# Tokens leave PSUM as two one-pass halves, and the spatial gate's product runs in three one-pass products

## The chip, the cores and the metric

The kernel runs on one core of one Trainium2 chip. The metric is device time in microseconds (us). The kernel before takes 4471.25 us, the median of 3 runs (4468.71 to 4473.4). The profiled execution took 4474.2 us, and its trace spans 4472.3 us.

## The reference

The reference is a small model on 1024 tokens of width 1024, all in f32: a first block with three mixers and an MLP, then an even layer, an odd layer, and a mixture of experts behind each. The change touches the stretch from the end of the first block's mixers to the projections of the even layer. In the reference's words:

```
x = x + gt_m * (merged @ w_out[l])
h = rms_norm(x, norm_mlp_g[l]) * (1.0 + sc_f) + sh_f
x = x + gt_f * (jnp.square(jax.nn.relu(h @ mlp_w1[l])) @ mlp_w2[l])
return rms_norm(x, final_norm_g)          # end of the first block
```

The even layer normalizes that x once more and multiplies it with one wide matrix. 512 of its columns go through a GELU and a spatial gate (a product over tokens), the other 2304 are the queries, keys and values of 12 attention heads, with a rotation of some columns. Both products take the same turned tokens h.

## The kernel before

**Stages.** The program is a row of stages. Each is a block with one instruction list per engine, written out in the order in which the engine runs it. `Stage.__exit__` (line 47) ends each with a barrier of all engines, so no engine starts a stage before the last engine has ended the one before. There is no scheduler: the source sets the order, and semaphores (`wait_ge`, `then_inc`) tie the engines.

**One product, two ways.** Tokens are turned by TensorE (a transpose of 128x128 tiles with the identity), since a product needs its contraction on the partitions. A product of f32 operands as they are is one `matmul` per tile. The other way is `split` (line 143) and `three_passes` (line 150): each operand is cast to fp32r (its high half) and the rest (its low half) is subtracted from it; then high times high, high times low and low times high are added up in PSUM, each with an fp32r `matmul`.

```
def three_passes(pe, out, left, right, start, stop):
    (lh, ll), (rh, rl) = left, right
    pe.matmul(out, lh, rh, start=start, stop=False)
    pe.matmul(out, lh, rl, start=False, stop=False)
    return pe.matmul(out, ll, rh, start=False, stop=stop)
```

**The stretch of the change**, stage by stage:

- `out_norm_stage` as "out" (lines 1725 to 1926): for each of 8 token tiles, 48 matmuls with `w_out`, the gate and the sum on VectorE, the norm, 8 transposes into PSUM (`out_th`), and a copy by ScalarE into `m["hT"]` as f32 (line 1857). The MLP's first weights are loaded here ahead of time (`mlp_ahead`).
- `mlp_stage` (lines 1942 to 2154): VectorE first splits the whole of `m["hT"]` (128x8192), then the first weights (128x4096), and TensorE waits for both (`h_split`, `w_split`). Then 8 turns, each with 8 tiles of `hidden` (24 matmuls) and 16 of `output` (12 matmuls). In the last turn the norms for the even layer ride along: `add`, `mean`, `inverse` on VectorE, squares and roots on ScalarE, 8 transposes for each token tile on TensorE (`turn_h`), and a copy by ScalarE into `m["hT"]` (lines 2078 and 2082).
- `spatial_stage` (lines 2157 to 2225): 8 tiles of 8 f32 matmuls each, `m["hT"]` times one weight slot of 128x4096 (line 2187), a GELU on ScalarE for each tile, then the norm of the gate on VectorE, four products over tokens (line 2195) and four gates.
- `gemm_stage` as "even" (lines 552 to 714): VectorE splits `m["hT"]` in four pieces and, after the first piece, the first of six sets of weights (128x3072 each), which is loaded at the start of this stage. TensorE runs 48 tiles of 24 matmuls of 384 columns, and turns queries and keys one tile late (line 647), when VectorE has rotated them (`x_ready`).

**Names.** `m["hT"]` and `m["hT_r"]`, `m["oN"]` and `m["oN_r"]`, `ring` and `ring_r` are each one piece of memory under an f32 and an fp32r name. The ring has four slots of 128x4096. SP's queue carries the loads, POOL's the stores.

## Time and profile before

| what | us |
|---|---|
| median of 3 runs | 4471.25 |
| the profiled execution | 4474.2 |
| its span in the trace | 4472.3 |
| TensorE busy, share of the span | 3847.5, 86% |
| VectorE busy | 2588.4, 58% |
| ScalarE busy | 1653.6, 37% |

The stretch of the change, from the trace (busy time inside each window):

| window, us from the start | what runs | TensorE busy | VectorE busy | ScalarE busy | granted clock |
|---|---|---|---|---|---|
| 1213 to 1326 | out | 98.67 | 65.29 | 34.48 | 0.94 |
| 1326 to 1347 | split of tokens and weights, MLP | 0.14 | 19.75 | 0.03 | 0.50 |
| 1347 to 2002 | the MLP up to its last outputs | 655.00 | 365.95 | 38.24 | 1.00 |
| 2002 to 2065 | last outputs with norms | 53.60 | 46.30 | 28.25 | 0.93 |
| 2065 to 2124 | spatial: the f32 product | 57.23 | 0.00 | 6.35 | 0.96 |
| 2124 to 2141 | spatial: the gate | 5.80 | 12.70 | 1.45 | 0.70 |
| 2141 to 2153 | split of tokens and weights, even | 0.00 | 8.29 | 0.00 | 0.68 |
| 2153 to 2370 | the even projections | 214.69 | 72.83 | 36.48 | 0.99 |

The granted clock is TensorE's, as a share of full speed (0.50 is 1.2 GHz, 1.00 is 2.4 GHz). Busy time tells which engine works; what ends a stretch is read from the idle time in front of an instruction and from the engine that ended it.

### The profile page before, as it was taken

How to read it: one execution, taken by the hardware profiler on the slowest of the kernel's cores; microseconds unless marked ns; L12 is line 12 of the kernel's file. 1: busy time of each engine (PE TensorE's matmuls, PEld its weight loads, DVE VectorE, ACT ScalarE, POOL GpSimd, SP SyncE). 2: the span in 40 equal slices, each digit the busy share in tenths (PEclk: the TensorE clock that was granted, in tenths of full speed). 3: DMA queues.
4: the chain of work that ended last, by engine and by line, in shares of the span. 5: the costliest groups of instructions: out<-in, count | busy, mean ns of one | idle time of the engine just before them, and what ended most of it. 6: DMA issues, size and time to landing. Idle time of an engine off the chain costs nothing. (4 is left out here: it accounts for less than half of the span.)

```text
span 4472.3 us, 56432 instructions
## 1 busy us (share of the span) xinstructions
PE 3847.5 (86%) x22256; PEld 3122.2 (70%) x22256; DVE 2588.4 (58%) x3982; ACT 1653.6 (37%) x2226; POOL 493.3 (11%) x471
## 2 busy tenths in 40 slices
PE   5988998977989999998797998599677798993996
PEld 2766877866767888885796876377566687872775
DVE  6356772068755555553524763677565465745775
ACT  2223342155420000003114762367513465732675
POOL 0001122000000000000230000133103000000341
PEclk9989999989999999999898999799888899996998
DMA  7101113230531111111313103399603202032997
GB/s 293 48 22 62 62 64 104 71 126 33 177 134 38 38 56 50 44 66 42 113 46 139 38 26 137 127 374 370 206 16 96 68 20 112 13 115 98 355 371 274
DMA packets 136489, 518.88 MB, mean 116 GB/s; under 512 B 17952, under 2 KB 70336, under 8 KB 118224
## 3 DMA queue, kind: packets, MB, share of 16 engines
q1 hardware_dynamic: 101936, 411.94, 25.1%
q0 software_dynamic: 31216, 101.85, 7.2%
q8 instruction: 149, 2.44, 0.2%
q10 hardware_dynamic: 3120, 2.10, 0.2%
q14 instruction: 68, 0.56, 0.0%
HBM read 427.21 MB, written 88.62 MB: 115 GB/s over the span
## 5 line engine op out<-in xcount | busy, mean ns | idle before, releaser
L2052 ACT ACTIVATE mlp_relu<-mlp_z 128x512 f32<-128x512 f32 x64 | 38.3, 598 | 637.7 <-PE mlp_z L155 637.7
L3106 DVE TENSOR_TENSOR ring_r<-ring,oN_r 128x4096 fp32r<-128x4096 f32 x48 | 212.2, 4424 | 67.8 <-ACT oN_r L3037 67.7
L153 PE MATMUL scans_G<-ring_r 128*128 128x512 f32 x544 | 221.8, 408 | 32.3 <-ACT scans_stg L2560 18.3
L3106 DVE TENSOR_TENSOR ring_r<-ring,hT_r 128x4096 fp32r<-128x4096 f32 x48 | 212.3, 4423 | 59.3 <-ACT hT_r L3037 59.3
L153 PE MATMUL mlp_z<-ring_r,mlp_w_high_r 128*128 128x512 f32 x512 | 200.0, 391 | 21.9 <-DVE ring_r L147 21.9
L3037 ACT ACTIVATE oN_r<-ring 128x4096 fp32r<-128x4096 f32 x48 | 174.0, 3629 | 82.2 <-DMA ring<-in_w_all 67.6
L3037 ACT ACTIVATE hT_r<-ring 128x4096 fp32r<-128x4096 f32 x48 | 174.0, 3628 | 70.2 <-DMA ring<-in_w_all 70.2
L155 PE MATMUL mlp_z<-ring_r 128*128 128x512 f32 x512 | 199.7, 390 | 0.0
L154 PE MATMUL mlp_z<-hT_r,mlp_w_high_r 128*128 128x512 f32 x512 | 199.6, 390 | 0.0
L153 PE MATMUL mlp_y_ps<-mlp_w_high_r,oN_r 128*128 128x512 f32 x512 | 199.6, 390 | 0.0
L155 PE MATMUL mlp_y_ps<-mlp_w_high_r,oN_r 128*128 128x512 f32 x512 | 199.2, 389 | 0.0
L154 PE MATMUL mlp_y_ps<-ring_r,oN_r 128*128 128x512 f32 x512 | 199.2, 389 | 0.0
L154 PE MATMUL scans_G<-hT_r,ring_r 128*128 128x512 f32 x480 | 191.7, 399 | 0.0
L155 PE MATMUL scans_G<-ring_r 128*128 128x512 f32 x480 | 191.1, 398 | 0.0
L2924 POOL TENSOR_TENSOR moe_taker<-moe_zero 128x1 f32<-128x1 f32 x64 | 135.9, 2124 | 438.4 <-ACT moe_y L3096 425.9
L2099 DVE TENSOR_TENSOR mlp_relu<-mlp_relu 128x512 f32<-128x512 f32 x64 | 44.2, 691 | 184.8 <-ACT mlp_relu L2052 184.8
L2110 DVE TENSOR_TENSOR mlp_y<-mlp_y_ps,mlp_gt 128x512 f32<-128x512 f32 x128 | 88.2, 689 | 103.6 <-PE mlp_y_ps L155 101.3
L153 PEld LDWEIGHTS scans_G<-ring_r 128*128 128x128 f32 x544 | 104.9, 193 | 59.1 <-issue 14.8
L153 PE MATMUL even_gemm_acc<-even_gemm_w_high,even_gemm_h_high 128*128 128x384 f32 x384 | 133.9, 349 | 13.4 <-DVE ring_r L147 13.4
L1257 DVE CUSTOM_DVE_ANT_0 even_sc<-even_scores,even_table 128x1024 f32<-128x1024 f32 x96 | 117.0, 1220 | 23.3 <-issue 23.3
L154 PE MATMUL even_gemm_acc<-ring_r,even_gemm_h_high 128*128 128x384 f32 x384 | 130.1, 339 | 0.0
L155 PE MATMUL even_gemm_acc<-even_gemm_w_high,hT_r 128*128 128x384 f32 x384 | 129.8, 338 | 0.0
(645 smaller groups left out, 10654.9 us busy)
## 6 DMA issues: line engine op xcount, KB each, us to landing
ring<-in_w_all SPq DMA_DIRECT2D x118, 2048.0 KB, 10.7
ring<-in_w_mlp SPq DMA_DIRECT2D x16, 2048.0 KB, 7.7
ring<-in_w_all SPq DMA_DIRECT2D x12, 1024.0 KB, 6.3
branch_gates<-scans_stg POOLq DMA_DIRECT2D x48, 256.0 KB, 2.3
merge_raw<-branch_gates SPq DMA_DIRECT2D x16, 768.0 KB, 5.1
ring<-in_w_even SPq DMA_DIRECT2D x6, 1536.0 KB, 8.2
qk_turned<-even_gemm_y POOLq DMA_DIRECT2D x48, 128.0 KB, 2.3
even_qk<-qk_turned SPq DMA_DIRECT2D x6, 1024.0 KB, 5.1
```

Source lines behind the costliest of these rows:

```text
L153: pe.matmul(out, lh, rh, start=start, stop=False)
L154: pe.matmul(out, lh, rl, start=False, stop=False)
L155: return pe.matmul(out, ll, rh, start=False, stop=stop)
L1257: dve.tensor_tensor_reduce(out=sc[:, u % 3, :], in0=SA[:, 2 * (u % 2):2 * (u % 2) + 2, :].rearrange("p a n -> p (a n)"), in1=table[:, c:c ...
L2052: act.activation(r[:, n % 2, :], Z[:, n % 4, :], ACT.Relu).then_inc(z_free, 1)
L2099: step(dve.tensor_tensor(r[:, n % 2, :], r[:, n % 2, :], r[:, n % 2, :], ALU.mult))
L2110: dve.tensor_tensor(y[:, n % 2, :], Y[:, n % 4, :], gt[:, cols], ALU.mult).then_inc(y_free, 1)
L2924: pool.tensor_tensor(taker[:, n:n + 1], zero[:], zero[:], ALU.add)
L3037: act.activation(w_high[n % RING], buf[:, (first + n) % RING, :], ACT.Copy).then_inc(w_cast, 1)
L3106: dve.tensor_tensor(buf_r[:, b, :], buf[:, b, :], w_high[n % RING].bitcast(F32), ALU.subtract)\
```

## The change

1. In "out" (`halves=True`), ScalarE casts the turned tile from PSUM to fp32r into `m["oN_r"]`, and VectorE subtracts that from PSUM into `m["hT_r"]` (`low_h`). The f32 copy goes away. The next transposes wait for VectorE now.
2. In `mlp_stage` the split of the tokens is gone. The first weights are split in four quarters, the cast on ScalarE and the rest on VectorE, and TensorE's first tile waits for a quarter at each second k. The hidden layer's halves lie in ring slots 2 and 3 (they were in `m["oN_r"]`).
3. In the last turn of the MLP the tokens leave PSUM as halves too: `cast_h` on ScalarE, `low_h` on VectorE.
4. `spatial_stage` takes these halves, splits its weight slot in four quarters on ScalarE and VectorE, and runs 24 fp32r matmuls per tile in place of 8 f32 ones. It also loads the even layer's first weights into ring slot 1.
5. `gemm_stage` is left for "even" alone. The split of the tokens is gone; the first weights, in memory by then, are split in two halves on ScalarE and VectorE. Two of four weight buffers are new memory (`even_more`).

The diff, cut to its core:

```diff
 # out_norm_stage, ScalarE
                 if t >= 2:
                     act.wait_ge(h_turned, t - 1)
-                    act.activation(m["hT"][:, :, toks(t - 2)], TH[:, :, :], ACT.Copy).then_inc(h_taken, 1)
+                    if halves:
+                        act.wait_ge(o_split, t - 1)
+                        act.activation(m["oN_r"][:, :, toks(t - 2)], TH[:, :, :], ACT.Copy).then_inc(h_cast, 1)
 ...
 # out_norm_stage, VectorE
+            def low_h(i):
+                dve.wait_ge(h_cast, i + 1)
+                dve.tensor_tensor(m["hT_r"][:, :, toks(i)], TH[:, :, :], m["oN_r"][:, :, toks(i)].bitcast(F32), ALU.subtract)\
+                   .then_inc(h_taken, 1)
 ...
                 if t + 1 < NT:
                     low_o(t + 1)
+                if halves and t >= 2:
+                    low_h(t - 2)
                 if t < NT:
                     add(t, 0)
+            if halves:
+                low_h(NT - 1)
 # mlp_stage, TensorE
-            pe.wait_ge(h_split, 1)
 ...
                     for k in range(KD):
+                        if n == 0 and k % 2 == 0:
+                            pe.wait_ge(first_split, k // 2 + 1)
 # mlp_stage, ScalarE
+            act.wait_ge(m["mlp_w_in"][0], 16)
+            for j in range(4):
+                act.activation(quarter(w_high, j), quarter(buf, j), ACT.Copy).then_inc(w_cast, 1)
 # mlp_stage, VectorE
-            split(step, dve, m["hT"][:, :, :], h_high, h_low[:, :, :]).then_inc(h_split, 1)
-            dve.wait_ge(m["mlp_w_in"][0], 16)
-            split(step, dve, buf[:, 0, :], w_high[:, 0, :], buf_r[:, 0, :]).then_inc(w_split, 1)
+            dve.nop().then_inc(w_split, 1)
+            for j in range(4):
+                dve.wait_ge(w_cast, j + 1)
+                dve.tensor_tensor(quarter(buf_r, j), quarter(buf, j), quarter(w_high, j).bitcast(F32), ALU.subtract)\
+                   .then_inc(first_split, 1)
             dve.wait_ge(x_in, 32)
 ...
                 if 1 <= t <= NT:
                     mean(t - 1, 1)
+                if t >= 3:
+                    low_h(t - 3)
 # spatial_stage
+            sp.dma_start(buf[:, 1, 0:EVEN_W], m["w_even"][0, :, :]).then_inc(m["even_in"], 16)
 ...
-                    ins = pe.matmul(Z[:, t % 4, :], m["hT"][:, k, t * P:(t + 1) * P], w[:, k, :],
-                                    start=k == 0, stop=k == KD - 1)
+                    if t == 0 and k % 2 == 0:
+                        pe.wait_ge(w_split, k // 2 + 1)
+                    ins = three_passes(pe, Z[:, t % 4, :], [h[:, k, t * P:(t + 1) * P] for h in (h_high, h_low)],
+                                       [v[:, k, :] for v in w], k == 0, k == KD - 1)
 # gemm_stage, VectorE
-            for q in range(4):
-                toks = slice(q * 2 * P, (q + 1) * 2 * P)
-                split(step, dve, m["hT"][:, :, toks], h_high[:, :, toks], h_low[:, :, toks]).then_inc(h_split, 1)
-                if q == 0:
-                    split_w(0)
+            for j in range(2):
+                dve.wait_ge(w_cast, j + 1)
+                dve.tensor_tensor(half(w_low[0], j), half(w_raw[0], j), half(w_high[:, 0, :], j).bitcast(F32), ALU.subtract)\
+                   .then_inc(first_split, 1)
```

VectorE's list from the last norm of "out" into the MLP (`out_h` is the normed tile, `hT_r` the low half of the tokens, `ring_r` in the first of these rows the high half), before:

```order
L1917 SCALAR_TENSOR_TENSOR out_h<-out_x,out_rs,out_gain 128x1024
L1921 TENSOR_TENSOR out_h<-out_h,out_shift 128x1024
L36 UNCONDITIONAL_BRANCH
L2084 UNCONDITIONAL_BRANCH
L146 CAST ring_r<-hT 128x8192
L147 TENSOR_TENSOR hT_r<-hT,ring_r 128x8192
L146 CAST mlp_w_high_r<-ring 128x4096
L147 TENSOR_TENSOR ring_r<-ring,mlp_w_high_r 128x4096
```

and with the change:

```order
L1898 SCALAR_TENSOR_TENSOR out_h<-out_x,out_rs,out_gain 128x1024
L1902 TENSOR_TENSOR out_h<-out_h,out_shift 128x1024
L1887 TENSOR_TENSOR hT_r<-out_th,oN_r 128x8x128 x2
L37 UNCONDITIONAL_BRANCH
L2083 UNCONDITIONAL_BRANCH
L2090 TENSOR_TENSOR ring_r<-ring,mlp_w_high_r 128x1024 x4
```

Two subtractions of one tile each stand before the stage's end, and four of a quarter behind it, in place of two instructions over all tokens and two over all of the weights.

VectorE's list at the end of the MLP (`mlp_w_high` is where the normed tile lies, `mlp_z` the PSUM of the transposes), before:

```order
L2117 TENSOR_SCALAR mlp_ss<-mlp_ss 128x1
L2122 RECIPROCAL mlp_rs<-mlp_rs 128x1
L2145 SCALAR_TENSOR_TENSOR mlp_w_high<-mlp_x,mlp_rs,mlp_w_high 128x1024
L36 UNCONDITIONAL_BRANCH
L2207 UNCONDITIONAL_BRANCH
L377 TENSOR_TENSOR spatial_sq<-spatial_z 128x2048
```

and with the change:

```order
L2118 TENSOR_SCALAR mlp_ss<-mlp_ss 128x1
L2139 TENSOR_TENSOR hT_r<-mlp_z,ring_r 128x8x128
L2123 RECIPROCAL mlp_rs<-mlp_rs 128x1
L2152 SCALAR_TENSOR_TENSOR mlp_w_high<-mlp_x,mlp_rs,mlp_w_high 128x1024
L2139 TENSOR_TENSOR hT_r<-mlp_z,ring_r 128x8x128 x2
L37 UNCONDITIONAL_BRANCH
L2229 UNCONDITIONAL_BRANCH
L2234 TENSOR_TENSOR ring_r<-ring,spatial_w_high 128x1024 x4
L378 TENSOR_TENSOR spatial_sq<-spatial_z 128x2048
```

One subtraction has come between the last mean and its reciprocal, two behind the last norm, and four quarters of weights into the stage that follows.

SP's queue where the spatial stage meets the even projections, before:

```order
L2176 DMA spatial_bs<-in_b_spatial 128x4
L36 UNCONDITIONAL_BRANCH
L587 UNCONDITIONAL_BRANCH
L592 DMA ring<-in_w_even 128x3072
L600 DMA even_gemm_cos<-in_cos_even 128x64
```

and with the change:

```order
L2190 DMA spatial_bs<-in_b_spatial 128x4
L2191 DMA ring<-in_w_even 128x3072
L37 UNCONDITIONAL_BRANCH
L579 UNCONDITIONAL_BRANCH
L582 DMA ring<-in_w_even 128x3072
L586 DMA even_gemm_cos<-in_cos_even 128x64
```

The first weights' load stands one stage earlier, and the second weights' load is the first of the stage now.

## Rows read from the trace of the kernel before

**Rows 1.** Timeline, out's end to MLP: start us, us, engine, line, tile [idle before <-releaser].

```profile
1305.02 0.69 DVE L1891 TENSOR_TENSOR out_h<-out_y_ps,out_gate 128x512 f32<-128x512 f32 x1 [3.11 <-PE out_y_ps L155]
1323.00 1.97 PE L1811 MATMUL out_th<-identity,out_h 128*128 128x128 f32 x8 [5.35 <-DVE out_h L1921]
1325.01 1.02 ACT L1857 ACTIVATE hT<-out_th 128x1024 f32<-128x1024 f32 x1 [4.83 <-PE out_th L1811]
1326.98 4.43 DVE L146 CAST ring_r<-hT 128x8192 fp32r<-128x8192 f32 x1 [4.04 <-PEq L39]
1331.45 8.69 DVE L147 TENSOR_TENSOR hT_r<-hT,ring_r 128x8192 fp32r<-128x8192 f32 x1
1342.38 4.42 DVE L147 TENSOR_TENSOR ring_r<-ring,mlp_w_high_r 128x4096 fp32r<-128x4096 f32 x1
1346.86 0.80 PE L153 MATMUL mlp_z<-ring_r,mlp_w_high_r 128*128 128x512 f32 x1 [21.88 <-DVE ring_r L147]
1348.30 0.63 PE L153 MATMUL mlp_z<-ring_r,mlp_w_high_r 128*128 128x512 f32 x1
1348.73 0.63 PE L154 MATMUL mlp_z<-hT_r,mlp_w_high_r 128*128 128x512 f32 x1
1354.08 0.60 ACT L2052 ACTIVATE mlp_relu<-mlp_z 128x512 f32<-128x512 f32 x1 [28.05 <-PE mlp_z L155]
1359.52 0.60 ACT L2052 ACTIVATE mlp_relu<-mlp_z 128x512 f32<-128x512 f32 x1 [4.84 <-PE mlp_z L155]
```

**Rows 2.** Timeline of the merge stage: prices of casts and subtractions.

```profile
1118.56 1.05 ACT L1373 ACTIVATE merge_w_high<-ring 128x1024 fp32r<-128x1024 f32 x1
1209.37 1.49 ACT L1385 ACTIVATE merge_raw<-merge_raw 128x1536 f32<-128x1536 f32 x1 [4.47 <-DMA merge_raw<-branch_gates]
1129.09 1.23 DVE L1398 TENSOR_TENSOR ring_r<-ring,merge_w_high 128x1024 fp32r<-128x1024 f32 x1
1130.23 1.22 DVE L1393 TENSOR_TENSOR hT_r<-merge_tp,merge_o_high 128x1024 fp32r<-128x1024 f32 x1
1131.37 0.68 DVE L1416 TENSOR_TENSOR oN<-merge_raw,merge_up 128x512 f32<-128x512 f32 x1
```

**Rows 3.** Issues of the MLP's start: KB, us from issue to landing.

```profile
mlp_x<-x_rows SPq DMA_DIRECT2D x1, 4096.0 KB, 13.1
```

**Rows 4.** Timeline, the last outputs of the MLP.

```profile
2042.30 0.69 DVE L2110 TENSOR_TENSOR mlp_y<-mlp_y_ps,mlp_gt 128x512 f32<-128x512 f32 x1 [1.15 <-PE mlp_y_ps L155]
2060.23 0.15 DVE L2117 TENSOR_SCALAR mlp_ss<-mlp_ss 128x1 f32<-128x1 f32 x1 [1.22 <-ACT mlp_relu L2062]
2060.66 0.16 DVE L2122 RECIPROCAL mlp_rs<-mlp_rs 128x1 f32<-128x1 f32 x1 [0.27 <-ACT mlp_rs L2067]
2064.20 1.02 ACT L2082 ACTIVATE hT<-mlp_z 128x1024 f32<-128x1024 f32 x1 [2.66 <-PE mlp_z L2030]
```

**Rows 5.** Timeline, the spatial product.

```profile
2066.01 1.28 ACT L2202 ACT_TABLE_LOAD   x1 [0.79 <-PEq L39]
2066.05 9.16 PE L2187 MATMUL spatial_z_ps<-ring,hT 128*128 128x512 f32 x16 [1.89 <-PEq L39]
2123.32 0.60 ACT L2202 ACTIVATE spatial_z<-spatial_z_ps 128x512 f32<-128x512 f32 x1 [6.27 <-PE spatial_z_ps L2187]
```

**Rows 6.** Timeline, the start of the even projections.

```profile
2141.57 1.23 DVE L146 CAST even_gemm_h_high<-hT 128x2048 fp32r<-128x2048 f32 x1 [0.77 <-PEq L39]
2153.45 0.66 PE L153 MATMUL even_gemm_acc<-even_gemm_w_high,even_gemm_h_high 128*128 128x384 f32 x1 [13.44 <-DVE ring_r L147]
2160.41 0.49 ACT L659 ACTIVATE oN<-even_gemm_acc 128x384 f32<-128x384 f32 x1 [31.29 <-PE even_gemm_acc L155]
2164.57 0.49 ACT L659 ACTIVATE oN<-even_gemm_acc 128x384 f32<-128x384 f32 x1 [3.67 <-PE even_gemm_acc L155]
2170.62 0.44 PE L647 MATMUL even_gemm_tp<-identity,oN 128*128 128x128 f32 x2 [1.40 <-DVEq L714]
```

**Rows 7.** Windows: us, PE, PEld, DVE, ACT, POOL busy, granted clock, DMA, GB/s.

```profile
2145.00:2146.00 1.00, 0.00 (x0) 0.00 (x0) 0.12 (x1) 0.00 (x0) 0.00 (x0) 0.65 1.09 467
```

More of the change, by code:

```diff
@@ L549, in take_turned, with gemm_stage @@
         act.activation(dst[:, ks, t * P:(t + 1) * P], psum[:, t % 2, ks, :], ACT.Copy).then_inc(free, 1)
-def gemm_stage(nc, m, kind):
-    with Stage(nc, f"{kind}_gemm") as st:
-        even = kind == "even"
-        NS, WIDE, NB = (6, 3 * P, 2) if even else (2, 3 * P + 64, 3)
+def gemm_stage(nc, m):
+    with Stage(nc, "even_gemm") as st:
+        NS, WIDE, NB = 6, 3 * P, 2
         N, SIZE, HEADS = NS * NT, KD * WIDE, 2 * NB
         VW = WIDE - NB * P
-        buf, buf_r = (t_[:, :, 0:SIZE] for t_ in (m["ring"].buf, m["ring"].buf_r))
-        h_high = st.sb("h_high", [P, KD, S], F32R)
-        h_low = m["hT_r"]
+        more, more_r = twin_buffer(nc, st.ctx, "even_more", [P, 2, SIZE])
+        w_raw, w_low = ([t_[:, b, 0:SIZE] for b in (1, 0)] + [u_[:, b, :] for b in range(2)]
+                        for t_, u_ in ((m["ring"].buf, more), (m["ring"].buf_r, more_r)))
+        h_high, h_low = ring_halves(m), m["hT_r"]
@@ L1722, in _, with out_norm_stage @@
             step(dve.tensor_tensor(o, sq, g_sub[:, :].unsqueeze(1).unsqueeze(1).to_broadcast([P, NT, H, P]), ALU.mult))
-def out_norm_stage(nc, m, name, src, gain, gate=None, scale=None, shift=None, turned=range(KD), keep=None, ahead=None, o_turned_in=None):
+def out_norm_stage(nc, m, name, src, gain, gate=None, scale=None, shift=None, turned=range(KD), keep=None, ahead=None, o_turned_in=None,
+                   halves=False):
     with Stage(nc, name) as st:
@@ L2199, in _ @@
         def _(act):
+            m["ring"].wait(act, first)
+            for j in range(4):
+                act.activation(quarter(w_high, j), quarter(buf[:, slot, :], j), ACT.Copy).then_inc(w_cast, 1)
             for t in range(NT):
@@ L2209, in _ @@
             step = Steps(dve, stepped)
+            for j in range(4):
+                dve.wait_ge(w_cast, j + 1)
+                dve.tensor_tensor(quarter(buf_r[:, slot, :], j), quarter(buf[:, slot, :], j),
+                                  quarter(w_high, j).bitcast(F32), ALU.subtract).then_inc(w_split, 1)
             dve.wait_ge(par_in, 48)
```

143 lines of the change are left out of this document (67 added, 76 removed).

## The prediction

> **What bounds the kernel now.** I read the page's busy shares first (the table ahead of this), then busy time by window, then the timeline of each engine around the four places the diff touches. The chain of waits is of no use here, since it names only the last stage. TensorE is busy 86% of the span. Inside the MLP, in "out" and in the even projections it hardly waits, so VectorE and ScalarE have room there and their work costs nothing. In three places TensorE stands and VectorE works alone. (a) Between "out" and the MLP TensorE waits 21.88 us, and what ends that wait is the last subtraction of the weights' split; before it VectorE has cast and subtracted all tokens, 4.43 and 8.69 us [rows 1]. (b) At the even projections it waits 13.44 us for the same kind of work [rows 6]. (c) Once more it waits 1.40 us for a rotated tile [rows 6]. A fourth place is of another kind: the f32 product of the spatial stage has TensorE busy from 2066.05 until the last GELU starts at 2123.32, 57.27 us [rows 5], with ScalarE and VectorE nearly idle. Between any two stages lies a barrier, so every microsecond at these places is a microsecond of the kernel.
>
> **The end of "out", +2.4 us.** Before, the last 8 transposes start at 1323.00, when the normed tile is ready, the copy starts at 1325.01 and takes 1.02, and the stage ends at 1326.03 [rows 1]. Now two subtractions of 128x1024 stand behind the last norm. The first belongs to tile 6, and the last transposes wait for it, since there is one buffer in PSUM. The subtraction of that very form, PSUM minus fp32r half, takes 1.22 us in the merge stage, and the next instruction starts 1.14 after it started [rows 2]. So the transposes start about 1.15 later; then come 2.01, the cast with 1.02, and the second subtraction with 1.22 plus a few hundredths for the handover. The stage ends at 1326.03 + 1.15 + 1.24, 2.39 later. The other six subtractions lie where VectorE waits for TensorE; in each round of "out" it waits 3.11 us (the row at 1305.02) [rows 1], and nothing that TensorE needs in that round comes later by more than the subtraction's 1.14.
>
> **The start of the MLP, -17.5 us.** Before: 20.83 us from the end of "out" (1326.03) to the first matmul (1346.86) [rows 1]. Now: the barrier, 0.95 (1326.03 to 1326.98) [rows 1]; ScalarE's cast of the first quarter, 128x1024, 1.05 [rows 2]; VectorE's subtraction, 1.23 [rows 2]; two handovers of about 0.05, of which the one to TensorE is read in [rows 1] (1342.38 + 4.42 to 1346.86). Together 3.3. The other quarters come every 1.14, and TensorE needs 6 matmuls at 0.43 for one at its low clock [rows 1], so it doesn't wait for them. The barrier is not removed. What is late next is the load of the MLP's x. It starts 2.4 later, with the stage, takes 13.1 us [rows 3], and VectorE waits for it ahead of its first square. So it is ready near 1343, some 3 to 4 us after the first relu (1331.8 + 7.22 = 1339.0, with 7.22 from the first matmul to the first relu [rows 1]). Behind this wait stand VectorE's splits of the hidden layer, and behind these ScalarE's third relu (two buffers are free at the start) and TensorE's seventh tile. Tiles come 5.44 apart (1354.08 to 1359.52) [rows 1], so TensorE asks for that at about 1331.8 + 7.2 + 5 x 5.44 = 1366. Cost nothing, with 20 us to spare.
>
> **The last turn of the MLP, +2.0 us.** VectorE gets one more subtraction in each of six rounds. In a full round it is idle for 1.15 us ahead of the next round's product (the row at 2042.30) [rows 4]. The step of 1.14 fits, with next to nothing left. I take 0; 0.3 a round (a step of 1.4) in five rounds would be 1.5 us. The Trainium skill speaks against a fit: "VectorE: DVE Perf Modes", the section on the TRN2 errata, gives a Vector instruction 120 cycles of fixed cost with a PSUM source and 58 with an SBUF source, 62 cycles at 0.96 GHz, 65 ns more. The trace does not bear that out for this form: 1.22 us from PSUM beside 1.23 from SBUF [rows 2]; by the rule the sum would change by no more than 0.3 us. At the end: the last mean starts at 2060.23, the reciprocal at 2060.66 [rows 4]. Now the subtraction of tile 5 comes between and holds VectorE until 2060.23 + 0.07 + 1.14 = 2061.44, so the last norm, transposes and cast come 0.78 later, and behind the cast (2064.20 + 1.02 [rows 4]) comes the last subtraction, 1.22 and a handover: 0.78 + 1.25 = 2.03.
>
> **The spatial product, -9.6 us.** A tile is now 24 fp32r matmuls of 512 columns, which is what a tile of the MLP's hidden layer is: 5.44 us, and 7.22 from the first matmul to the first relu, with the slow clock of the start in it [rows 1]. Eight tiles: 7.22 + 7 x 5.44 = 45.3, in place of 57.27. The stage also starts with a quarter's cast and subtraction ahead of TensorE, 2.33 (its weights have been in memory since the MLP). -11.97 + 2.33 = -9.64. The GELU's table load of 1.28 [rows 5] moves behind the casts and stays hidden by the first tile. The gate behind it is untouched. The slow start could be as long as that of the even projections, whose first tile takes 6.96 and the second 4.16 [rows 6], 2.8 more; in the MLP it is 1.8 more. So -8.6 is the other end.
>
> **The even projections, -8.5 and -1.4 us.** Before: 11.88 us from the stage's first instruction (2141.57) to the first matmul (2153.45) [rows 6]. Now ScalarE casts a half of 128x1536: 1.49, by the activation of that size, and VectorE subtracts it: 1.23 for 1024 and 4.42 for 4096 columns [rows 1, 2] give 1.76 for 1536. With handovers 3.34. -8.54. The load of these weights lies in the spatial stage, beside 45 us of matmuls. The second half is ready 1.8 us after the first, and TensorE needs 12 matmuls for the first, about 3.5 us. The wait of 1.40 [rows 6] came from VectorE being busy with tokens until after the first tile; now the first rotation starts when its tile is there, and the split of the second weights, 5.1 us long, ends about a microsecond before TensorE asks for the second rotated tile (after its third tile, 2 x 4.16 behind the first). Gone: -1.40, at worst 0. The load of the second weights is issued at the stage's start and has landed by then, as the first weights had in 6.6 us before. One thing can give more: in the window 2145 to 2146 the granted clock falls, 0.65 on average [rows 7], and TensorE's first matmul would now come at 2144.9 on this time scale. If the clock holds, the slow start goes, up to 2.5 us of the 2.8. I leave it in, since the fall and the start are within half a microsecond.
>
> **The sum.** 2.4 - 17.5 + 2.0 - 9.6 - 8.5 - 1.4 = -32.6 us. Against its own time of 4474.2 the profiled execution would take 4441.6; it stands 3.0 above the median of the runs (4471.25), and the same difference against the median gives 4438.6. I say 4439 us, 0.73% faster. About 0.2%, 9 us, is what a measurement of this kernel can tell from no change.
>
> **Rivals.**
> - *VectorE bounds the MLP's last rounds, and the slow starts are long.* For it: 1.14 into 1.15 us. Against: the step is measured on the same form. It gives +1.5, +1.0 in the spatial product, and the 1.40 stays: 4442.5.
> - *The clock holds into the even projections.* -2.5: 4436. For it: TensorE's matmuls of the gate end nearly 5 us before, and the fall comes just then. Against: the fall comes first if nothing else sets it.
> - *The waits move rather than go.* The splits go, but TensorE then stands for the MLP's x, or for weights that have not landed, for 10 to 15 us more. Against: the room of 20 us above, weights loaded a stage ahead. It would give about 4450.
> - *Slower: TensorE stays at its low clock.* With shorter pauses and more matmuls the granted clock might not rise in the spatial product and the first of the even weight sets. Price: a matmul of 512 columns 0.43 apart (1348.30 to 1348.73 [rows 1]) in place of 0.227 (5.44 / 24), 0.20 more, for 192 of them +39; and 192 of 384 columns at about 0.15 more, +28. That gives 4438.6 + 67 less the slow starts counted already, about 4502. It decides from about 160 matmuls at the low clock against the gain of 32.6, and 205 for slower by over 0.2%. Against: at each start in this trace the clock rises within the first tile.
> - *The change doesn't do what it says*, for example VectorE is still what TensorE waits for because quarters come too slowly: each would cost at most 0.1 us by the steps above.
>
> **How the numbers follow.** Forecast 62%, with its own range 4434 to 4444 (measurement 2.5 either way, 2 for the ends of the terms); VectorE and long starts 12%, clock holds 15%, waits moved 8% (half of it within the range below), low clock 3%. Range 4431 to 4448: it leaves out the worst of the moved waits, the low clock and a tail on the fast side, under 2 in 10. Faster by over 0.2% (under 4462): 0.94; within: 0.03; slower by over 0.2%: 0.03.
>
> **What would show it.** TensorE's wait ahead of the MLP's first matmul falls from 21.9 to about 5.7, with the transposes' wait ahead of it up from 5.35 to 6.5; 13.4 ahead of the even projections becomes about 5; the spatial product's last GELU starts some 45 us after its first matmul; no wait of 1.4 at the second turned tile; VectorE's idle time in the MLP's last rounds near zero at an unchanged distance of rounds. I am wrong if the rounds of "out" or of the MLP's last turn grow longer, if TensorE waits for a hidden tile's relu in the first turn, or if a stage that the diff does not touch moves.

## The result, and the profile after

The changed kernel takes 4441.36 us, the median of 4 runs (4439.74 to 4450.08), beside 4472.32 for the kernel before (4 runs, 4468.71 to 4478.27). The ratio is 0.9933, with a 95% interval of 0.9916 to 0.9951. The forecast was 4439, range 4431 to 4448. The profiled execution took 4439.74 us. Its page says of span and busy time:

```profile
span 4437.9 us, 56597 instructions
PE 3831.2 (86%) x22320; PEld 3131.0 (71%) x22320; DVE 2581.3 (58%) x3994; ACT 1662.6 (37%) x2236; POOL 499.9 (11%) x471
```

The shares are those of before. What moved can be seen only at the four places. Timeline of the changed kernel from the end of "out" into the MLP (start us, us, engine, line, tile, then the idle time before and what ended it), the counterpart of [rows 1]:

```profile
1319.96 1.94 PE L1783 MATMUL out_th<-identity,out_h 128*128 128x128 f32 x8 [6.58 <-DVE hT_r L1887]
1321.93 1.02 ACT L1831 ACTIVATE oN_r<-out_th 128x1024 fp32r<-128x1024 f32 x1 [6.03 <-PE out_th L1783]
1322.99 1.23 DVE L1887 TENSOR_TENSOR hT_r<-out_th,oN_r 128x1024 fp32r<-128x1024 f32 x1 [3.18 <-ACT oN_r L1831]
1325.08 3.90 ACT L2044 ACTIVATE mlp_w_high_r<-ring 128x1024 fp32r<-128x1024 f32 x4 [2.13 <-PEq L40]
1326.17 4.63 DVE L2090 TENSOR_TENSOR ring_r<-ring,mlp_w_high_r 128x1024 fp32r<-128x1024 f32 x4 [1.96 <-ACT mlp_w_high_r L2044]
1327.54 0.77 PE L154 MATMUL mlp_z<-oN_r,mlp_w_high_r 128*128 128x512 f32 x1 [5.65 <-DVE ring_r L2090]
1339.49 0.69 DVE L2100 TENSOR_TENSOR mlp_relu<-mlp_relu 128x512 f32<-128x512 f32 x1 [8.69 <-DMA mlp_gt<-mod_rows]
```

TensorE waited 21.88 us ahead of the MLP's first matmul and now waits 5.65. Its last transposes waited 5.35 and now wait 6.58, for the subtraction that the change put ahead of them. The last row is the wait for the MLP's x and gate.

Timeline of VectorE in one of the MLP's last rounds, and of the stage's end, the counterpart of [rows 4]:

```profile
2008.36 0.15 DVE L2118 TENSOR_SCALAR mlp_ss<-mlp_ss 128x1 f32<-128x1 f32 x1
2008.43 1.21 DVE L2139 TENSOR_TENSOR hT_r<-mlp_z,ring_r 128x1024 fp32r<-128x1024 f32 x1
2009.67 0.69 DVE L2111 TENSOR_TENSOR mlp_y<-mlp_y_ps,mlp_gt 128x512 f32<-128x512 f32 x1
...
2041.30 1.22 DVE L2139 TENSOR_TENSOR hT_r<-mlp_z,ring_r 128x1024 fp32r<-128x1024 f32 x1
2042.43 0.15 DVE L2123 RECIPROCAL mlp_rs<-mlp_rs 128x1 f32<-128x1 f32 x1
2042.62 1.28 DVE L2152 SCALAR_TENSOR_TENSOR mlp_w_high<-mlp_x,mlp_rs,mlp_w_high 128x1024 f32<-128x1024 f32 x1
2047.02 1.23 DVE L2139 TENSOR_TENSOR hT_r<-mlp_z,ring_r 128x1024 fp32r<-128x1024 f32 x1 [1.98 <-ACT ring_r L2068]
```

The subtraction of 1.21 stands where VectorE was idle for 1.15, and the product behind it (2009.67) starts with no bracket, so with no idle time. At the end the subtraction at 2041.30 stands between the mean and its reciprocal.

Timeline of the spatial product, the counterpart of [rows 5]:

```profile
2051.46 0.79 PE L154 MATMUL spatial_z_ps<-spatial_w_high,ring_r 128*128 128x512 f32 x1 [5.53 <-DVE ring_r L2234]
2096.97 0.60 ACT L2224 ACTIVATE spatial_z<-spatial_z_ps 128x512 f32<-128x512 f32 x1 [4.84 <-PE spatial_z_ps L156]
```

From its first matmul to its last GELU are 45.5 us instead of 57.3. Timeline and windows (us; PE, PEld, DVE, ACT and POOL busy; granted clock) of the start of the even projections, the counterpart of [rows 6, 7]:

```profile
2119.05 0.66 PE L154 MATMUL even_gemm_acc<-even_gemm_w_high,ring_r 128*128 128x384 f32 x1 [4.96 <-DVE ring_r L672]
2125.43 0.49 ACT L651 ACTIVATE oN<-even_gemm_acc 128x384 f32<-128x384 f32 x1 [6.94 <-PE even_gemm_acc L156]
2129.60 0.49 ACT L651 ACTIVATE oN<-even_gemm_acc 128x384 f32<-128x384 f32 x1 [3.67 <-PE even_gemm_acc L156]
```

```profile
2115.00:2116.00 1.00, 0.00 (x0) 0.00 (x0) 0.00 (x0) 0.37 (x1) 0.00 (x0) 1.00 0.00 0
2116.00:2117.00 1.00, 0.00 (x0) 0.00 (x0) 0.00 (x0) 1.00 (x1) 0.00 (x0) 0.70 0.70 123
2117.00:2118.00 1.00, 0.00 (x0) 0.00 (x0) 0.85 (x1) 1.00 (x2) 0.00 (x0) 0.50 0.52 184
```

The wait of 13.44 is 4.96, and no turned tile is waited for. In the MLP's last turn the transposes of two neighbouring tiles are 6.81 us apart, as before, and the tiles of "out" 11.8 us, as before: the rounds did not grow. The clock falls between 2116 and 2117, before the first matmul at 2119.05.

**A table of steps.** The stretch of the change can be cut at instructions that all kernels have. The numbers are differences of start times (an end, where it says end) in the profiled executions, in us:

| from the row before to | before | after | predicted change | measured change |
|---|---|---|---|---|
| end of "out", from ScalarE's take of tile 6 (counted from 0) | 8.34 | 10.80 | +2.39 | +2.46 |
| MLP's first matmul | 20.83 | 3.32 | -17.5 | -17.51 |
| first relu | 7.22 | 7.53 | 0 | +0.31 |
| last relu | 647.36 | 647.36 | 0 | 0 |
| end of the MLP | 63.78 | 65.82 | +2.03 | +2.04 |
| last GELU | 58.10 | 48.72 | -9.64 | -9.38 |
| end of the gate | 17.47 | 17.91 | 0 | +0.44 |
| first even matmul | 12.66 | 4.17 | -8.54 | -8.49 |
| first copy of an even tile | 6.96 | 6.38 | 0 | -0.58 |
| fifth copy | 19.32 | 17.48 | -1.40 | -1.84 |
| last copy | 189.77 | 189.77 | 0 | 0 |
| sum | 1051.81 | 1019.26 | -32.6 | -32.55 |

The rest of the kernel, span less sum, is 3420.5 before and 3418.6 after: no instruction was changed there. The difference of the medians is 31.0 us. That the two sums agree to 0.1 us is luck: single steps are off by up to 0.6 either way and cancel.

### The profile page after: what moved, and what is told of

It reads as the page before. It is cut to its first block and busy times, and to the rows that moved or that the text cites. A ratio compares the mean times of both kernels' runs of the same rounds, so it can differ in the third digit from the quotient of the medians.

```text
span 4437.9 us, 56597 instructions
## 1 busy us (share of the span) xinstructions
PE 3831.2 (86%) x22320; PEld 3131.0 (71%) x22320; DVE 2581.3 (58%) x3994; ACT 1662.6 (37%) x2236; POOL 499.9 (11%) x471
## 5 line engine op out<-in xcount | busy, mean ns | idle before, releaser
L154 PE MATMUL mlp_z<-oN_r,mlp_w_high_r 128*128 128x512 f32 x512 | 200.0, 391 | 5.6 <-DVE ring_r L2090 5.6
L156 PE MATMUL mlp_z<-oN_r,ring_r 128*128 128x512 f32 x512 | 199.8, 390 | 0.0
L154 PE MATMUL mlp_y_ps<-mlp_w_high_r,ring_r 128*128 128x512 f32 x512 | 199.6, 390 | 0.0
L156 PE MATMUL mlp_y_ps<-mlp_w_high_r,ring_r 128*128 128x512 f32 x512 | 199.2, 389 | 0.0
L155 PE MATMUL mlp_y_ps<-ring_r 128*128 128x512 f32 x512 | 199.2, 389 | 0.0
L154 PE MATMUL even_gemm_acc<-even_gemm_w_high,ring_r 128*128 128x384 f32 x384 | 133.7, 348 | 5.0 <-DVE ring_r L672 5.0
L1181 ACT ACTIVATE even_sc<-even_sc,even_nm 128x1024 f32<-128x1024 f32 x96 | 110.0, 1145 | 23.4 <-DVE even_nm L1227 21.8
```

What stands on the lines that cost most here:

```text
L1181: act.activation(sc[:, u % 3, :], sc[:, u % 3, :], ACT.Exp, bias=nm[:, u % 4:u % 4 + 1], scale=-1.0, accum_out=rs[:, u % 8:u % 8 + 1]).the ...
```

## Experiments

Two theories stood against each other. Mine: the gain is the time in which VectorE worked alone at three stage starts, plus a cheaper form of one product, each to be read from its stage. The rival: a part of it is something else, the spread between executions (the stages ahead of the change were 4.3 us earlier in the profiled run of after), the clock at the starts, or a wait that only moved. Each kernel was read by the same steps (us; the sum is over the whole stretch, "rest" is span less sum):

```
                         before  after     x1     x2     x3     x4     x5     x6     x7     x8     x9    x10
end of "out"               8.34  10.80  10.80  10.80  10.79  10.80  10.79   9.93   9.60   8.74   8.73  10.79
MLP's first matmul        20.83   3.32   3.32   7.79   3.33   3.33   3.33   4.06   3.33   3.63   3.33   3.33
first relu                 7.22   7.53   7.85   8.61   7.82   7.83   7.51   6.24   8.27   6.70   7.27   7.88
last relu                647.36 for all twelve
end of the MLP            63.78  65.82  63.78  65.81  65.83  65.83  73.90  64.95  65.07  64.19  64.13  65.79
last GELU                 58.10  48.72  58.49  49.28  59.12  48.87  49.70  47.07  49.44  47.08  48.36  48.89
end of the gate           17.47  17.91  17.66  18.25  17.98  18.02  17.04  15.64  18.37  15.64  15.63  18.02
first even matmul         12.66   4.17  12.62   4.18   4.17  10.78   4.17   4.67   4.17   4.66   4.66   4.17
first copy                 6.96   6.38   7.06   6.51   6.41   6.52   7.28   4.47   6.59   4.46   4.48   6.44
fifth copy                19.32  17.48  19.25  17.48  17.46  17.46  17.48  17.46  17.48  17.48  17.47  17.46
last copy                189.77, within 0.03, for all
sum                      1051.8 1019.3 1038.0 1025.8 1030.0 1026.5 1028.3 1011.6 1019.5 1009.7 1011.2 1019.9
rest                     3420.5 3418.6 3415.7 3416.2 3417.0 3424.0 3413.4 3420.4 3432.3 3422.7 3422.8 3426.1
```

### x1: the first two parts alone

The kernel before, with "out" and the MLP's start as changed, the MLP's tail, the spatial product and the even projections as they were.

```diff
 # mlp_stage of the changed kernel, ScalarE; VectorE's low_h is gone
-                act.activation(next_high[:, :, t * P:(t + 1) * P], TH[:, t % 2, :, :], ACT.Copy).then_inc(h_cast, 1)
+                act.activation(m["hT"][:, :, t * P:(t + 1) * P], TH[:, t % 2, :, :], ACT.Copy).then_inc(h_taken, 1)
```

> The change's first two parts alone: in 'out' the tokens leave PSUM as two halves, and the MLP's first weights are split in quarters. The MLP's last turn, the spatial product and the even projections are as before the change. Theory (the gain is the time in which VectorE worked alone, stage by stage): +2.4 at the end of 'out', -17.5 at the MLP's start, 15.1 under the kernel before: about 4457. In the trace TensorE's wait ahead of the MLP's first matmul is 5.6 to 5.7 instead of 21.9, and the spatial product and the even start have their old waits (13.4 and 1.4). Rival (4 of the 32.5 us are the spread between executions, since stages ahead of the change were 4.3 us earlier in the profiled run): the ratio shows a gain of 11 or less, or the stages ahead of 'out' come earlier in this kernel too.

Measured: 4455.56 us (5 runs), ratio 0.9961 [0.9948, 0.9975] to before, 15.7 under the median of before (4471.27, 9 runs). Timeline of TensorE at the MLP's first matmul:

```profile
1330.92 0.76 PE L154 MATMUL mlp_z<-oN_r,mlp_w_high_r 128*128 128x512 f32 x1 [5.65 <-DVE ring_r L2121]
```

"Out" ends 2.46 later and the MLP starts 17.51 sooner, to the hundredth as in the full change. All other steps keep their old values but for those that follow a pause (7.85 instead of 7.22, 58.49 instead of 58.10, 17.66 instead of 17.47). So this half is worth 15.0 us less these starts, 13.8 in the sum. The rival named the spread between executions. It is real, but it lies outside the stretch: "rest" is 4.8 shorter here than before, and the same steps inside come out the same. A single profiled span can't measure a part this small; the steps can.

### x2: the MLP's first weights whole, on VectorE

```diff
-            for j in range(4):
-                dve.wait_ge(w_cast, j + 1)
-                dve.tensor_tensor(quarter(buf_r, j), quarter(buf, j), quarter(w_high, j).bitcast(F32), ALU.subtract)\
-                   .then_inc(first_split, 1)
+            dve.wait_ge(m["mlp_w_in"][0], 16)
+            split(step, dve, buf[:, 0, :], w_high[:, 0, :], buf_r[:, 0, :]).then_inc(w_split, 1)
```

> The changed kernel, with the MLP's first weights cast and subtracted whole on VectorE as before the change (the tokens' split stays gone). Theory: TensorE's first matmul comes 0.95 + 2.2 + 4.42 + 0.05 = 7.6 us after the end of 'out' instead of 3.3, so +4.3 against the changed kernel (about 4445.7); the tokens' part of the 17.5 us is then 13.2. Rival (the quarters buy nothing, since the matmuls at the low clock are fed no faster, or since VectorE's later work becomes late): +1 or less, with a longer wait for the first relus or for the MLP's x in the changed kernel.

Measured: 4445.43 us, ratio 0.9943 [0.9930, 0.9957] to before. Timeline, VectorE and TensorE:

```profile
1324.24 2.29 DVE L147 CAST mlp_w_high_r<-ring 128x4096 fp32r<-128x4096 f32 x1 [0.98 <-PEq L40]
1326.57 4.43 DVE L148 TENSOR_TENSOR ring_r<-ring,mlp_w_high_r 128x4096 fp32r<-128x4096 f32 x1
1331.05 0.80 PE L154 MATMUL mlp_z<-oN_r,mlp_w_high_r 128*128 128x512 f32 x1 [10.11 <-DVE ring_r L148]
```

The first matmul comes 7.79 after the end of "out" instead of 3.32, +4.47 (7.6 was expected). So 4.5 of the 17.5 us come from the quarters and the second engine, and 13.0 from the tokens, which no longer have to be split. The rival (+1 or less) is out. The first relu came 1.1 later than in the changed kernel (8.61 beside 7.53). That the longer pause is the cause is not shown: the kernel before, after a pause of 21.88 us, had 7.22.

### x3: the spatial product as f32 again

The tokens' low half is left out of this product, and the weights are not split; count and size of the matmuls are those of before.

```diff
-                    ins = three_passes(pe, Z[:, t % 4, :], [h[:, k, t * P:(t + 1) * P] for h in (h_high, h_low)],
-                                       [v[:, k, :] for v in w], k == 0, k == KD - 1)
+                    ins = pe.matmul(Z[:, t % 4, :], h_high[:, k, t * P:(t + 1) * P].bitcast(F32), w[:, k, :],
+                                    start=k == 0, stop=k == KD - 1)
```

> The changed kernel with the spatial product as one f32 matmul for each k, of the tokens' high half and the unsplit weights (the tokens' low half is left out of this product; the number and the size of the matmuls are those of before the change). Theory: an f32 matmul of 512 columns takes 0.86 us a k beside 0.68 for three one-pass products, and the stage starts 2.3 us sooner: from the stage's start to the last GELU 58.1 instead of 48.7, +9.4 against the changed kernel (about 4450.8). Rival (a part of the 9.4 comes from the state in which TensorE enters the stage, clock or pauses, and not from the form of the product): +5 or less.

Measured: 4449.74 us, ratio 0.9949 [0.9936, 0.9963] to before. Timeline, the last GELU:

```profile
2110.52 0.60 ACT L2220 ACTIVATE spatial_z<-spatial_z_ps 128x512 f32<-128x512 f32 x1 [6.27 <-PE spatial_z_ps L2205]
```

The step is 59.12 us instead of 48.72, +10.4, a microsecond more than expected, since this time the start at the low clock was longer. With the low clock set aside, a tile takes 6.27 + 0.60 = 6.87 us by the row, the changed kernel's 4.84 + 0.60 = 5.44. So the form of the product gives the gain, 8 x 1.43 = 11.4, less 2.3 for the weights' split ahead of it. The rival (5 or less) is out.

### x4: the even layer's first weights loaded in their own stage

```diff
 # spatial_stage
-            sp.dma_start(buf[:, 1, 0:EVEN_W], m["w_even"][0, :, :]).then_inc(m["even_in"], 16)
 # gemm_stage
+            load(0)
             load(1)
```

> The changed kernel, with the even layer's first weights loaded at the start of the even projections instead of in the spatial stage. Theory (the early load carries part of the 8.5 us): the weights land 6.6 us after their issue, ScalarE's cast starts then, and the first matmul comes that much later: +6.5 against the changed kernel (about 4447.9), TensorE's wait 11.4 instead of 5.0; the wait of 1.4 at the second turned tile stays away. Rival (the load is short or lands in the barrier's shadow, so it matters little): +3 or less. Second rival: the wait of 1.4 at the turned tile hangs on when the second weights land, and comes back.

Measured: 4452.29 us, ratio 0.9955 [0.9941, 0.9968] to before. Timeline, ScalarE and TensorE:

```profile
2128.08 2.85 ACT L645 ACTIVATE even_gemm_w_high<-ring 128x1536 fp32r<-128x1536 f32 x2 [19.59 <-DMA ring<-in_w_even]
2131.50 0.66 PE L154 MATMUL even_gemm_acc<-even_gemm_w_high,ring_r 128*128 128x384 f32 x1 [11.57 <-DVE ring_r L673]
```

TensorE waits 11.57 instead of 4.96, and the step grows by 6.61: the load is worth that much of the 8.5 us. With the tokens' split gone but the load in its place, the gain here would have been 1.9. And that 1.9 does not come from the tokens. In the kernel before, VectorE was done with its first piece of tokens while the load was still under way, and waited for the load:

```profile
2148.19 1.76 DVE L146 CAST even_gemm_w_high<-ring 128x3072 fp32r<-128x3072 f32 x1 [3.07 <-DMA ring<-in_w_even]
```

From this cast to the first matmul (2153.45) were 5.26 us, all of it the weights' split on VectorE. Here, from ScalarE's cast (2128.08) to the first matmul (2131.50), they are 3.42: the weights' split in halves on two engines gives 1.84 of the 1.88. At this start the tokens' split cost TensorE next to nothing; it cost the wait at the turned tile. The fifth copy comes as in the changed kernel (17.46), so the wait at the turned tile does not come back: the second rival is out. The median is 10.9 above the changed kernel's. In the profiled executions the stretch is 7.3 longer, and "rest" 5.3: the larger figure holds a part that no edit made.

### x5: the MLP's last subtractions twice

```diff
             def low_h(t):
                 dve.wait_ge(h_cast, t + 1)
+                step(dve.tensor_tensor(h_low[:, :, toks], TH[:, t % 2, :, :], next_high[:, :, toks].bitcast(F32),
+                                       ALU.subtract))
```

> The changed kernel with each subtraction of the low half in the MLP's last turn done twice. Theory (the one subtraction a round used up VectorE's idle time of 1.15 us, nothing is left): each of the five rounds that hold one grows by up to 1.2 us, and the three behind the last outputs cost 1.2 each where they lie on the chain (two of them): from the last relu to the end of the MLP +6.0 + 2.4 = +8.4 against the changed kernel's 65.82 (about 74.2; 4450 in all). Rival (VectorE has more room in the rounds than its waits show, since four PSUM buffers lie between it and TensorE): only the end pays, +2.4 (68.2).

Measured: 4450.95 us, ratio 0.9956 [0.9942, 0.9969] to before. Timeline of VectorE and TensorE in the same round:

```profile
2008.17 1.21 DVE L2139 TENSOR_TENSOR hT_r<-mlp_z,ring_r 128x1024 fp32r<-128x1024 f32 x1
2009.42 1.22 DVE L2141 TENSOR_TENSOR hT_r<-mlp_z,ring_r 128x1024 fp32r<-128x1024 f32 x1
2010.56 0.68 DVE L2111 TENSOR_TENSOR mlp_y<-mlp_y_ps,mlp_gt 128x512 f32<-128x512 f32 x1
...
2013.48 1.09 PE L2021 MATMUL mlp_z<-identity,mlp_w_high 128*128 128x128 f32 x8 [1.38 <-DVE mlp_w_high L2154]
2021.44 1.09 PE L2021 MATMUL mlp_z<-identity,mlp_w_high 128*128 128x128 f32 x8 [1.40 <-DVE mlp_w_high L2154]
```

From last relu to the end: 73.90, +8.08 (74.2 expected, 68.2 by the rival). TensorE's transposes are 7.96 us apart instead of 6.81 (2026.22 to 2033.03 in the changed kernel; 2024.80 to 2031.61 in the one before), and wait 1.4 for VectorE instead of 0.25. The second subtraction has no room at all. So the first one filled the idle time to the last tenth, and the forecast's zero was right with nothing to spare.

### x6: spare matmuls in TensorE's waits

```diff
+def keep_clock(pe, out, src, count):
+    for _ in range(count):
+        pe.matmul(out, src[:, 0:P], src[:, 0:HALF], start=True, stop=True)
 # spatial_stage, and so at the other places named
+            keep_clock(pe, M[:, 1, :], h_high[:, 0, :], 42)
             pe.wait_ge(v_ready, 1)
```

> The changed kernel with spare fp32r matmuls of 512 columns (results unused) in TensorE's waits: 24 ahead of the last transposes of 'out' and 6 behind them, 9 at the MLP's start, 14, 10 and 6 around the last two transposed tiles of the MLP, 9 at the start of the spatial product, 42 ahead of the gate's products and 6 behind them, 13 at the start of the even projections. Theory (slow starts are the low clock alone, and work holds the clock): end of 'out' 10.80 to 9.9; MLP's first matmul to first relu 7.5 to 5.8; end of the MLP 65.82 to 64; stage start to last GELU 48.7 to 47.1; gate 17.9 to 16.4; first even matmul to first copy 6.4 to 4.3. Sum -9, about 4432. Rival (the clock falls at these places whatever TensorE does, for instance at each barrier): the spare matmuls take 0.43 us each, 9 of them 3.9 instead of 2.0, TensorE is 1.5 late at each of the three starts: +4, about 4445.

Measured: 4434.88 us, ratio 0.9919 [0.9906, 0.9933] to before. Windows of this kernel at the end of "out" and the MLP's start (columns as above):

```profile
1322.00:1324.00 2.00, 2.00 (x14) 1.71 (x13) 0.00 (x0) 1.03 (x1) 0.00 (x0) 1.00 0.00 0
...
1326.00:1327.00 1.00, 0.86 (x4) 0.76 (x5) 0.00 (x0) 0.88 (x1) 0.00 (x0) 1.00 0.00 0
1327.00:1328.00 1.00, 1.00 (x4) 0.76 (x3) 0.79 (x1) 1.00 (x2) 0.00 (x0) 0.54 1.03 119
1328.00:1329.00 1.00, 1.00 (x4) 0.77 (x3) 1.00 (x2) 1.00 (x3) 0.00 (x0) 0.50 0.81 319
```

and TensorE at its gate and the even start:

```profile
2094.73 9.68 PE L1922 MATMUL spatial_mixed<-ring_r 128*128 128x512 f32 x42
2105.83 3.95 PE L2232 MATMUL spatial_mixed<-spatial_z,spatial_ws 128*128 128x512 f32 x8 [1.41 <-DVE spatial_z L2264]
2111.93 3.21 PE L1922 MATMUL even_gemm_tp<-ring_r 128*128 128x512 f32 x13 [0.75 <-PEq L40]
```

The theory holds at four places of six. The gate's products take 3.95 us instead of 6.24, the first even tile 4.47 instead of 6.38, the spatial product 47.07 instead of 48.72, the end of "out" is 0.87 shorter. The end of the MLP is 0.87 shorter too, where I had put 1.8: the transposes of each of its last two tiles take 1.09 us instead of 1.97, and the step gained that difference once, since the last tile's still start when VectorE has its norm ready, 10.93 us after those of the third last tile in both kernels (2033.51 to 2044.44, and 2033.03 to 2043.96). At the MLP's start the clock fell, although TensorE had worked up to 1.8 us before and was working again: 9 spare matmuls took 3.37 us, the first matmul came 0.74 late, and the first relu 0.55 sooner in all. The sum is 7.6 shorter than the changed kernel's, against 9 expected. The rival (the clock falls whatever TensorE does) is out at four places and stands at the MLP's start. Behind the gate I had put too much: the 6 spare ones end 0.6 us after VectorE, and the step to the first even matmul is 0.5 longer.

### x7: second PSUM buffers

```diff
 # out_norm_stage, TensorE: tiles alternate between two PSUM buffers
-                    pe.wait_ge(h_taken, t)
+                    pe.wait_ge(h_taken, t - halves)
 # mlp_stage: tile 7 in the outputs' PSUM; the last three low halves behind the last norm
-                if t >= 3:
+                if 3 <= t < NT:
                     low_h(t - 3)
+                if t == NT + 1:
+                    low_h(NT - 3)
+                    low_h(NT - 2)
+                    low_h(NT - 1)
```

> The changed kernel with a second PSUM buffer for the turned tokens in 'out' (so that the last transposes don't wait for the subtraction of the tile before), and the MLP's last token tile turned into the outputs' PSUM, with the subtraction of its fifth tile (counted from 0) behind the last norm. Theory: the subtraction that I put on the chain leaves it: -1.15 at the end of 'out' (10.80 to 9.65) and -0.78 at the end of the MLP (65.82 to 65.04): about 4439.5. Rival (something else orders them, as ScalarE's cast or two engines reading PSUM at the same time): 0 to -0.4.

Measured: 4443.18 us, ratio 0.9934 [0.9920, 0.9948] to before. Timeline, the last transposes of "out":

```profile
1330.32 1.97 PE L1784 MATMUL out_tp<-identity,out_h 128*128 128x128 f32 x8 [5.35 <-DVE out_h L1903]
```

Their wait is 5.35 again, as in [rows 1], and for the normed tile. The two steps gain 1.20 and 0.75, against 1.15 and 0.78: the two terms of the forecast were where I had put them. The sum does not show it (1019.5 beside 1019.3), since this execution met longer low-clock starts, 8.27 and 49.44. Nor do the medians (4443.18 beside 4441.36): a gain of 1.9 us is below what these runs can tell, and only the steps show it.

### x8 and x9: both together, and with other counts

> Both of the last two edits in one kernel: spare matmuls in TensorE's waits, and the second PSUM buffers. Theory: the two gains add, -9 - 1.9 = -11, about 4430.5. Rival (with the second buffers TensorE waits less, so that the same 24 and 14 spare matmuls push the transposes back): the end of 'out' is no shorter than with the spare matmuls alone.

Measured: 4432.61 us, ratio 0.9907 [0.9891, 0.9922] to before. The end of "out" is 8.74 and that of the MLP 64.19, shorter than with either edit alone, so the gains add there. The sum is 9.5 under the changed kernel's, against 11 expected, and 42.1 under before's. x9 has these counts instead:

```diff
-            keep_clock(pe, Y[:, 0, :], h_high[:, 0, :], 9)
+            keep_clock(pe, Y[:, 0, :], h_high[:, 0, :], 5)
-                keep_clock(pe, TPW, w_high[:, 0, :], 6)
+                keep_clock(pe, TPW, w_high[:, 0, :], 9)
-            keep_clock(pe, TP[:, 1, :], h_high[:, 0, :], 13)
+            keep_clock(pe, TP[:, 1, :], h_high[:, 0, :], 11)
```

> The kernel with spare matmuls and second PSUM buffers, with 5 spare matmuls in place of 9 at the MLP's start, 9 in place of 6 behind the last transposes of 'out', and 11 in place of 13 at the even start. Theory: 9 were too many at the MLP's start, where the clock fell under them (3.63 us from the end of 'out' to the first matmul instead of 3.32), and 13 at the even start (4.66 instead of 4.17): -0.3 and -0.4, and with three more behind the transposes the clock holds into the MLP (first matmul to first relu from 6.70 to 5.8): -1.5 in all, about 4431. Rival (the clock falls at this start whatever TensorE did before): first matmul to first relu 7.0 to 7.5, 0 in all.

Measured: 4432.66 us, ratio 0.9911 [0.9897, 0.9924] to before. Window of x9 at the MLP's first matmul (1330.45):

```profile
1330.00:1331.00 1.00, 0.55 (x1) 0.50 (x2) 1.00 (x2) 1.00 (x2) 0.00 (x0) 0.62 0.84 336
```

The first matmul is on time again (3.33), and the clock falls just then, so the first relu takes 7.27: the rival's number. The step to the even start did not change (4.66): the 6 spare matmuls behind the gate were the cause there, not the 13. The sum came out 1.5 longer than x8's, where 1.5 less was expected. Most of that (1.28) is the spatial product, whose counts are those of x8: here the clock fell at its start too. I have not found counts that hold the clock into the MLP.

### x10: the MLP's x loaded twice

```diff
             sp.dma_start(x[:], m["x1"].rearrange("(t p) d -> p t d", p=P)).then_inc(x_in, 16)
+            sp.wait_ge(x_in, 16)
+            sp.dma_start(x[:], m["x1"].rearrange("(t p) d -> p t d", p=P)).then_inc(x_in, 16)
```

> The changed kernel with the MLP's x loaded twice, one load behind the other, so that VectorE's first square comes some 13 us later (near 1352.5 on the changed kernel's time scale instead of 1339.5). Theory (as predicted: TensorE asks for the third relu only near 1362, so there is room): first to last relu unchanged but for the first relus, TensorE's first matmul to last relu +0. Rival (behind the six squares stands the split of the second weights, 6.7 us, which TensorE needs after its eighth tile, near 1373; 1352.5 + 6 x 2.1 + 6.7 = 1371.8, more with the waits for the relus between): TensorE waits 0 to 3 us ahead of its first output tile, and the MLP grows by as much.

Measured: one run, 4447.76 us. Timeline, VectorE's first square and its split of the second weights, and ScalarE's eighth relu:

```profile
1356.10 0.69 DVE L2102 TENSOR_TENSOR mlp_relu<-mlp_relu 128x512 f32<-128x512 f32 x1 [21.45 <-DMA mlp_gt<-mod_rows]
1371.52 4.43 DVE L148 TENSOR_TENSOR ring_r<-ring,mlp_w_high_r 128x4096 fp32r<-128x4096 f32 x1
1377.34 0.60 ACT L2051 ACTIVATE mlp_relu<-mlp_z 128x512 f32<-128x512 f32 x1 [4.84 <-PE mlp_z L156]
```

The first square comes 24.7 us after the first matmul instead of 12.0, and the MLP does not grow (first to last relu 647.36): x is not late, by at least 12.8 us. But the room is not 20. The split of the second weights ends at 1375.95, and TensorE is done with the eighth tile at 1377.3, 1.4 us later. About 14 us (12.8 + 1.4) is all there is, by an estimate from these rows; no run delays x so far that TensorE waits.

## Why the prediction was right

- **Which places count.** Right. The stages' inner parts stand still to 0.03 us (647.36, 189.77), and all of the change lies where TensorE stood, as the idle times in front of three matmuls had said. One of them was read short. At the even projections VectorE did not work through the whole wait: for 3.07 us it waited for the weights' load itself, and its first piece of tokens lay beside that load (x4).
- **The starts, -17.5 and -8.5.** Right in size, and x2 and x4 show what they are made of: 13.0 for the tokens and 4.5 for the quarters at the MLP, 1.9 for the weights' split in halves and 6.6 for the earlier load at the even projections. In the prediction the load was part of one sum; alone it is the larger share.
- **What was added, +2.4 and +2.0.** Right; x7 took 1.20 and 0.75 of it back by the means that the mechanism named. x5 shows that the zero for the rounds had no reserve.
- **The spatial product, -9.6.** Mechanism right, measured -9.38. The gate behind it, held to be untouched, took 0.44 more. In the nine executions without spare matmuls it took 17.04 to 18.37 and with them 15.64, so 0.44 is within what the low clock does there.
- **The rule of the Trainium skill weighed at the MLP's last turn.** "VectorE: DVE Perf Modes", the section on the TRN2 errata, gives 120 cycles of fixed cost with a PSUM source and 58 with an SBUF source, by an estimate from these 65 ns more. The trace of after does not show it: 1.21 to 1.23 us from PSUM (the rows at 2008.43 and 2047.02), and 1.22 from SBUF (the four quarters at 1326.17 by their mean, 1221 ns).
- **The turned tile, -1.4.** The wait is gone; the four tiles gained 1.84. The rest is mostly that the first turned tile had been late too. From a tile's last matmul to the transposes behind it before had 0.39 us (2164.20 to 2164.59) and then 1.74 (2168.88 to 2170.62); after has 0.18 both times (2129.22 to 2129.40, 2133.63 to 2133.81). That is 1.77.
- **The clock at the even start.** The rival "it holds" is out: the granted clock was 0.50 before the first matmul. The first tile still took 0.58 less, because the low clock ended sooner, some 4.2 us after the first matmul instead of 5.5 (granted clock 0.88 from 2123 to 2124; before, 0.53 from 2158 to 2159). The rival of a clock that stays low is out by the same rows, and in the spatial product by 1.00 from 2055 to 2056, four microseconds behind its first matmul. Over the nine executions of the MLP's start without spare matmuls (before and after among them, and x2 with its longer pause), first matmul to first relu took 7.2 to 8.6 us, the spatial step in its new form 48.7 to 49.7. The forecast allowed up to 1.0 more in the spatial product and up to 2.5 less at the even start, nothing at the MLP's start, and kept zero in the sum; the three starts came to +0.31 (MLP), a part of the spatial term's +0.26, and -0.58 (even). What sets the length of such a start stays open.
- **A size that was off.** The room for the MLP's x was put at 20 us, because I followed the wait only to the third relu. The nearer need is the split of the second weights behind six tiles of VectorE's work. x10 puts the room at 14. It cost nothing, since 3 to 4 were needed.
- **What I said would prove me wrong.** Stages outside did move: they are 1.9 us shorter in after, and over the twelve profiled executions "rest" went from 3413.4 to 3432.3 with the same instructions. In x7 VectorE's first subtraction of the stage near 830 us came at 836.98 instead of 828.57, and the merge stage's at 1118.12 instead of 1108.81, both ahead of any edit. That sign was badly chosen, since it comes with every execution. What sets it stays open.

The likeliest case was forecast at 4439, and came at 4441.4 against a before that had risen from 4471.25 to 4472.3 in the median. Against that, 32.6 less is 4439.7.

## What to carry to other kernels

Where two stages meet at a barrier, look for the engine that works alone there: a conversion that the next stage needs can cost its full length there (13.0 us at the MLP), while the same conversion tile by tile inside the stage before cost only what stands behind the last norm (2.46 us, and 1.26 with a second PSUM buffer), as long as that engine has idle time in each round (here 1.15 us for 1.14). Look first whether that engine itself waits for a load: at the even projections the tokens' first piece lay beside the load and cost next to nothing. Split the first weights so that the consumer can start on a piece (4.5 us at the MLP, 1.9 at the even projections), and load them a stage ahead (6.6 us at the even projections; the MLP's were ahead already). And judge changes of a few microseconds by steps between instructions that both kernels have: steps that follow no pause agreed to hundredths, and those that do to about a microsecond, where whole runs differed by ten microseconds.

## What the hardware did that I had not expected

- **An f32 matmul costs less than four one-pass ones.** Per k, 6.87 / 8 = 0.859 us for one f32 matmul of 512 columns, and 5.44 / 8 = 0.680 for three fp32r ones, 0.227 each. The Trainium skill's "FP8 and Floating Point Precision", section "TensorE Precision Notes", counts 4 passes for true FP32. Four times 0.227 would be 0.907, so the trace agrees with four passes only if a pass inside an f32 matmul takes 0.215. The three-pass form gains 21%, not 25%.
- **The clock can fall under work, and not every time.** In x6 TensorE had paused 1.8 us at the barrier and was some 0.9 us into new matmuls when the granted clock went from 1.00 to 0.50. At the spatial start x6 and x9 have the same spare matmuls and the same pause, and the clock stayed at 1.00 in x6 (and in x8) but fell in x9, under work again (the timeline of TensorE and a window of each, x6 first):

```profile
2048.72 2.28 PE L1922 MATMUL spatial_mixed<-ring_r 128*128 128x512 f32 x9 [1.80 <-PEq L40]
2049.00:2050.00 1.00, 1.00 (x6) 0.81 (x5) 0.20 (x1) 1.00 (x2) 0.00 (x0) 1.00 0.31 101
...
2050.09 3.85 PE L1923 MATMUL spatial_mixed<-ring_r 128*128 128x512 f32 x9 [1.79 <-PEq L40]
2050.00:2051.00 1.00, 0.92 (x3) 0.81 (x4) 0.00 (x0) 0.94 (x1) 0.00 (x0) 0.73 0.01 2
2051.00:2052.00 1.00, 1.00 (x3) 0.74 (x3) 0.85 (x1) 1.00 (x3) 0.00 (x0) 0.50 0.80 184
```

  Without spare matmuls the same pause gave starts of different length: 7.51 to 8.27 us at the MLP after 5.65 us, 48.72 to 49.44 at the spatial product after 5.53.
- **Spare matmuls pay.** 139 of them, whose results nobody reads, took 7.6 us off the stretch by the steps of x6 (the medians, 4434.88 beside 4441.36, are too close to show it by themselves), mostly where a few f32 products or a first tile follow a long wait: 6.24 to 3.95 us for the gate's products.
